# A two-block model on one core: six of nine norms scale the products instead of the operand, and the down projection lags two chunks

## What is computed

```python
def rms_norm(x, g):
    y = xf * lax.rsqrt(jnp.mean(xf * xf, axis=-1, keepdims=True) + EPS)
    return (y * g).astype(x.dtype)

def conv_ffn(h, w_up, conv_w, conv_b, w_down):   # block 1, twice (FFN 0 and 1)
    u = h @ w_up                                 # 256 x 5632
    u = conv(u, conv_w, 3 taps along tokens) + conv_b
    a, b = u[..., :D_FF], u[..., D_FF:]
    return (jax.nn.silu(a) * b) @ w_down         # D_FF = 2816

def _swiglu(x, w_in, w_out):                     # block 2, twice (FFN 2 and 3)
    gate, up = jnp.split(x @ w_in, 2, axis=-1)
    return (jax.nn.silu(gate) * up) @ w_out
```

## Time and profile before

| what | value |
|---|---|
| time, median of 3 runs | 1320.73 us (1319.76 to 1320.78) |
| span of the profiled execution, first to last instruction | 1316.1 us |
| what lies around the span (median less span) | 4.6 us |
| PE busy | 1248.9 us, 95% of the span |
| DVE busy | 844.6 us, 64% |
| ACT busy | 662.6 us, 50% |
| mean granted TensorE clock | 0.978 of full speed |

### The profile page before, as it was taken

The page is one execution under the profiler, slowest core; times in us unless marked ns, Lnnn a source line. Parts: engine busy times, 40 slices in busy tenths (PEclk is TensorE's granted clock), DMA queues, the critical chain, the costliest instruction groups (busy, mean ns, idle before and its releaser), DMA issues.

```text
span 1316.1 us, 21598 instructions
## 1 busy us (share of the span) xinstructions
PE 1248.9 (95%) x8351; PEld 1140.8 (87%) x8360; DVE 844.6 (64%) x1556; ACT 662.6 (50%) x1156; POOL 3.5 (0%) x9
## 2 busy tenths in 40 slices
PE   6999789999999889999999999999999899999996
PEld 6999768999998667899999799999899679999984
DVE  7877947666667845666766655554778855555563
ACT  6745435555546643555555534443667134344452
POOL 0000000000000000000000000000000000000000
PEclk9999979999999979999999999999999999999998
DMA  8534403554455212255455454455543134444540
GB/s 346 199 134 145 147 30 144 191 191 182 175 188 207 111 49 96 101 201 184 186 191 192 147 207 179 185 191 191 189 148 144 49 120 183 176 178 183 189 144 32
DMA packets 20433, 211.40 MB, mean 161 GB/s; under 512 B 2400, under 2 KB 2400, under 8 KB 3360
## 3 DMA queue, kind: packets, MB, share of 16 engines
q1 hardware_dynamic: 20016, 208.90, 42.9%
q0 software_dynamic: 368, 1.84, 0.4%
HBM read 209.68 MB, written 1.05 MB: 160 GB/s over the span
## 4 chain that ended last, share of the span: by engine, by line
PE 86%; DVE 8%; ACT 4%; issue 1%; DMA 1%; SPq 0%; ACTq 0%; DVEq 0%
PE ps L305 25%; PE ps L306 25%; PE ps L307 25%; PE ps L310 10%; DVE w_lo L1233 2%; ACT w_hi L812 1%; ACT arena L812 1%; DMA raw<-in_stream 1%; ACT arena L847 1%; DVE x L1299 1%; DVE arena L1729 0%; PE ps L633 0%; PE ps L468 0%; DVE arena L1323 0%; DVE arena L1547 0%
## 5 line engine op out<-in xcount | busy, mean ns | idle before, releaser
L1233 DVE TENSOR_TENSOR w_lo<-raw,w_hi 128x1024 fp32r<-128x1024 f32 (+1 forms) x390 | 444.7, 1167 | 41.3 <-ACT w_hi L812 40.6
L305 PE MATMUL ps<-h_hi,w_hi 128*128 128x256 f32 x1608 | 456.0, 284 | 0.2 <-DVE h_lo L1286 0.2
L307 PE MATMUL ps<-h_hi,w_lo 128*128 128x256 f32 x1608 | 455.0, 283 | 0.0
L306 PE MATMUL ps<-h_lo,w_hi 128*128 128x256 f32 x1608 | 455.0, 283 | 0.0
L812 ACT ACTIVATE w_hi<-raw 128x1024 fp32r<-128x1024 f32 (+1 forms) x390 | 379.1, 1007 | 6.0 <-PE ps L307 4.6
L305 PEld LDWEIGHTS ps<-h_hi,w_hi 128*128 128x128 f32 x1608 | 308.3, 192 | 3.5 <-issue 0.3
L306 PEld LDWEIGHTS ps<-h_lo,w_hi 128*128 128x128 f32 x1608 | 308.3, 192 | 3.2
L307 PEld LDWEIGHTS ps<-h_hi,w_lo 128*128 128x128 f32 x1608 | 308.3, 192 | 0.0
L305 PE MATMUL ps<-w_hi,y_hi 128*128 128x512 f32 (+2 forms) x550 | 212.1, 386 | 12.3 <-DVE y_lo L1342 5.0
L306 PE MATMUL ps<-w_lo,y_hi 128*128 128x512 f32 (+2 forms) x550 | 210.4, 382 | 0.0
L307 PE MATMUL ps<-w_hi,y_lo 128*128 128x512 f32 (+2 forms) x550 | 209.3, 381 | 0.0
(11 more groups left out here) (275 smaller groups left out, 1037.9 us busy)
## 6 DMA issues: line engine op xcount, KB each, us to landing
raw<-in_stream SPq DMA_DIRECT2D x130, 1536.0 KB, 6.3
x<-in_x SPq DMA_DIRECT2D x1, 1024.0 KB, 4.9
arena<-in_mem SPq DMA_DIRECT2D x1, 1024.0 KB, 11.9
x<-in_x POOLq DMA_DIRECT2D x1, 1024.0 KB, 5.7
out<-arena SPq DMA_DIRECT2D x4, 256.0 KB, 2.5
vec<-in_vectors SPq DMA_DIRECT2D x1, 893.0 KB, 6.6
arena<-in_final POOLq DMA_DIRECT2D x1, 512.0 KB, 5.6
arena<-in_masks SPq DMA_DIRECT2D x1, 352.0 KB, 12.0
```

Source lines behind the costliest of these rows:

```text
L305: pe.matmul(o, lh, rh, start=start, stop=False, skip_group_check=True)
L306: pe.matmul(o, lh, rl, start=False, stop=False, skip_group_check=True)
L307: return pe.matmul(o, ll, rh, start=False, stop=stop, skip_group_check=True)
L1233: dve.tensor_tensor(w_lo[:, s, a], raw[:, s, a], w_hi[:, s, a], ALU.subtract).then_inc(s_lo, 1)
```

## The change

For norms 1, 2, 3, 4, 6 and 7 (`LATE`) PE transposes `x` as it is (`turn`), in four groups, each as soon as DVE has added its part; ACT and DVE split `x * gain`; the factor is computed behind that. In an FFN the factor is spread over the partitions by two small products (`spread`, copied by ACT to `rb`), and DVE multiplies each `up` product by it (`tu`, two instructions of 128 x 256 for a chunk); convolution, silu and gate then read `tu` in SBUF instead of PSUM. After norm 2 and in the last stage the factor is the `scale` of ACT's copies and sigmoids, which were there before. `warm` and the zero products that cleared the four banks go with these six norms. Norms 0, 5 and 8 stay. In the FFNs `down` comes one chunk later (up(3), down(1), up(4), down(2), ...; after the last `up`, three downs stand instead of two). The four sums end in the order of `LAST`; in an output projection's last group the fourth sum stands behind the first `turn`. Piece 0 of a unit's weights is split one chunk earlier than before, piece 2 waits for `unit_used` by itself.

```diff
+        LATE, EARLY = (1, 2, 3, 4, 6, 7), (0, 5, 8)
+        LAST = ((0, 0), (1, 0), (0, 1), (1, 1))
+        XT_BANK = (7, 5, 6, 0)
...
 def norm(i):                                   # PE; now for 0 and 5 only
                 if i:
                     warm(WARM)
-                if i in FFN_NORM:
-                    pe.wait_ge(sem("x_done"), 4 * i)
-                    for b in range(4):
-                        full(ps[:, b, :], zero[:, :], zero[:, 0:1].to_broadcast([P, 512]))
...
 def kt_major(u, ah, al, ready, banks=(0, 1, 2, 3), norm=None):
+                        if k == KT - 1:
+                            m.then_inc(s_used if n == 3 else sem("sum_ready"), 1)
+                            if norm is not None and n == 2:
+                                turn(norm, 0)
...
+            def turn(i, n):
+                t, half = LAST[n]
+                pe.wait_ge(sem("x_done"), 4 * (i - 1) + n + 1)
+                if i == 7 and n == 0:
+                    pe.wait_ge(sem("pleT_done"), 1)
+                for k in range(4 * half, 4 * half + 4):
+                    m = pe.transpose(ps[:, XT_BANK[k // 2], ...], x[:, t, k * P:(k + 1) * P], ident)
+                    if t and k % 2:
+                        m.then_inc(sem("xT_ready"), 1)
+
+            def spread(i):
+                pe.wait_ge(sem("late_factors"), LATE.index(i) + 1)
+                for t in range(T):
+                    m = full(ps[:, 7, t * P:(t + 1) * P], NORM[:, t:t + 1].to_broadcast([P, P]), ident)
+                m.then_inc(sem("rb_ready"), 1)
...
 def ffn(i):                                    # PE
-                up(None, 0, FFN_NORM[i])
+                first_up()                     # both halves on each pair of h
+                spread(FFN_NORM[i])
+                up(None, 1)
+                up(None, 2)
+                down(None, 0)
-                with pe.Fori(0, (CH - 1) // 3) as r:
-                    for j in range(1, 4):
+                with pe.Fori(0, (CH - 4) // 3) as r:
+                    for j in range(3, 6):
                         up(r, j)
-                        down(r, j)
+                        down(r, j - 2)
+                up(None, CH - 1)
...
-                down(None, CH)
+                down(None, CH - 3)
+                down(None, CH - 2)
+                down(None, CH - 1)             # turn(0) stands before its fourth sum
+                if FFN_NORM[i] + 1 in LATE:
+                    for n in range(1, 4):
+                        turn(FFN_NORM[i] + 1, n)
...
 def late_norm(i, gain):                        # ACT
+                for n in range(3):
+                    square(n)
+                for k in range(4):
+                    high(k)
+                square(3)
+                for k in range(4, KT):
+                    high(k)
...
 def body(r, j):                                # DVE, one chunk
+                    for z in range(2):
+                        dve.tensor_tensor(tu[:, g, z * S:(z + 1) * S], ps[:, b, z * S:(z + 1) * S], rb,
+                                          ALU.mult).then_inc(sem("tu_done"), 1)
-                                m = dve.scalar_tensor_tensor(c, ps[:, b, z * S:(z + 1) * S - d], w, c,
+                                m = dve.scalar_tensor_tensor(c, tu[:, g, z * S:(z + 1) * S - d], w, c,
+                        lo(r, U0 + j + 2, 1)
                     dve.wait_ge(sem("silu_done"), at(r, n0 + j + 1))
                     dve.tensor_tensor(gg[:, g, :], sa[:, g, :], other, ALU.mult)
+                    lo(r, U0 + j + 2, 2)
                     dve.wait_ge(sem("g_hi_done"), at(r, n0 + j + 1))
                     dve.tensor_tensor(y_lo[:, g, :], gg[:, g, :], y_hi[:, g, :], ALU.subtract)
+                    lo(r, U0 + j + 3, 0)
...
 # last stage, PE
-            pe.wait_ge(sem("x_done"), 4 * 7)
...            # the small projection, now between the turns and the gate
-            norm(7)
-            pe.wait_ge(s_evac, EV[U_PROJ])
-            kt_major(U_GATE, h_hi, h_lo, lambda k: pe.wait_ge(sem("hT_ready"), 4 * 7 + k // 2 + 1))
+            pe.wait_ge(sem("hT_ready"), 4 * 7 + 4)
+            kt_major(U_GATE, h_hi, h_lo, lambda k: None, GATE_BANKS)
```

More of the change, by code:

```diff
@@ L378, in lo_at, with up_part, up @@
                     return 3 * (U0 + j) + p + 1 if r is None else r * 9 + (3 * (U0 + j) + p + 1)
-                def up(r, j, norm=None):
-                    s = (U0 + j) % SLOTS
+                def up_part(j, z, k):
+                    s, a = (U0 + j) % SLOTS, slice(z * PIECE + k * P, z * PIECE + k * P + P)
+                    return three(ps[:, 4 + j % 3, z * S:(z + 1) * S], w_hi[:, s, a], w_lo[:, s, a],
+                                 h_hi[:, k, :], h_lo[:, k, :], k == 0, k == KT - 1)
+                def up(r, j):
                     for z in range(2):
@@ L384, in up, with first_up @@
                         for k in range(KT):
+                            m = up_part(j, z, k)
+                    m.then_inc(sem("up_ready"), 1)
+                def first_up():
+                    pe.wait_ge(s_lo, lo_at(None, 0, 1))
+                    s = U0 % SLOTS
+                    for k in range(KT):
+                        if k % 2 == 0:
+                            pe.wait_ge(sem("hT_ready"), 4 * FFN_NORM[i] + k // 2 + 1)
+                        for z in range(2):
                             a = slice(z * PIECE + k * P, z * PIECE + k * P + P)
-                            if norm is not None and z == 0 and k % 2 == 0:
-                                pe.wait_ge(sem("hT_ready"), 4 * norm + k // 2 + 1)
@@ L395, in down @@
-                    pe.wait_ge(s_lo, lo_at(r, j, 2))
-                    pe.wait_ge(sem("g_lo_done"), n0 + j if r is None else r * 3 + (n0 + j))
-                    for t in range(T):
+                    s, g = (U0 + j + 1) % SLOTS, j % 3
+                    pe.wait_ge(s_lo, lo_at(r, j + 1, 2))
+                    pe.wait_ge(sem("g_lo_done"), n0 + j + 1 if r is None else r * 3 + (n0 + j + 1))
+                    for n, (t, half) in enumerate(LAST):
                         tt = slice(t * P, (t + 1) * P)
[L400 to L405, removed]
@@ L406, in down @@
-                    m.then_inc(s_used, 1)
-                up(None, 0, FFN_NORM[i])
-                pe.wait_ge(s_lo, lo_at(None, 0, 2))
-                full(ps[:, 7, 0:1], zero[:, :], zero[:, 0:1]).then_inc(s_used, 1)
-                with pe.Fori(0, (CH - 1) // 3) as r:
-                    for j in range(1, 4):
+                        a = slice(2 * PIECE + half * 512, 2 * PIECE + half * 512 + 512)
+                        m = three(ps[:, 2 * t + half, :], y_hi[:, g, tt], y_lo[:, g, tt],
+                                  w_hi[:, s, a], w_lo[:, s, a], j == 0 and r is None, True)
@@ L595, in _ @@
                     m.then_inc(sem("yT_ready"), 1)
-            kt_major(U_OUT0, y_hi, y_lo, beside_memory(0))
-            norm(1)
+            kt_major(U_OUT0, y_hi, y_lo, beside_memory(0), norm=1)
             ffn(0)
[L601 to L604, removed]
+            rows(U_MLA, 0, 384, (1, 2), h_hi, h_lo, norm=2).then_inc(s_used, 1)
+            rows(U_MLA + 1, 0, 320, (3, 4), h_hi, h_lo).then_inc(s_used, 1)
+            rows(U_MLA + 2, 0, MEM_W, (5, 0), h_hi, h_lo).then_inc(s_used, 1)
             pe.wait_ge(sem("c_done"), 1)
@@ L679, in _ @@
                     head_O(i - 3)
-            kt_major(U_OUT1, y_hi, y_lo, beside_memory(1))
-            norm(3)
+            kt_major(U_OUT1, y_hi, y_lo, beside_memory(1), norm=3)
             ffn(1)
-            norm(4)
             ffn(2)
@@ L783, in gla_y @@
                 pe.wait_ge(sem("y_ready"), KT * 2 + k + 1)
-            kt_major(U_OUT2, y_hi, y_lo, gla_y)
-            norm(6)
+            kt_major(U_OUT2, y_hi, y_lo, gla_y, norm=6)
             ffn(3)
-            pe.wait_ge(sem("pleT_done"), 1)
-            pe.wait_ge(sem("x_done"), 4 * 7)
             s = U_PROJ % SLOTS
@@ L896, in ffn @@
                     body(None, j)
-                for p in range(2):
-                    hi(None, U0 + CH + 1, p)
             def mem_kT(l):
@@ L1237, in split, with rsqrt @@
                     lo(None, u, p)
-            def rsqrt(out_, mean, n, t1, t2, scale=1.0):
+            def rsqrt(out_, mean, n, t1, t2, scale=1.0, done=None):
                 if mean is not None:
```

286 lines of the change are left out of this document (166 added, 120 removed).

## The result

The kernel after takes **1285.01 us** (median of 4, 1281.11 to 1286.43) against 1320.76 of the kernel before in the same session: a ratio of 0.9726, 95% interval 0.9713 to 0.9739, so 2.7% faster. The forecast was 1289.5, with 1278 to 1303 as its range.

The account below looks back on a forecast made before the run. PE was taken to bound the kernel inside an FFN. 13.9 + 14.7 + 6.4 - 0.4 - 3.4 = 31.2 off the span of 1316.1 gives 1284.9; plus 4.6 around it, 1289.5 us, range 1278 to 1303.

Parts of the forecast that it names:

- What bounds the kernel; the steady part: Inside an FFN PE is the bound; DVE's longer body takes 7.3 of a chunk's 8.5 us, so 0 change.
- Norms 1, 3 and 6: Behind an output projection: `up(1)` starts 4.3 us earlier at each; with 0.5 for two first downs, 13.9 gained.
- Norms 2 and 4: Behind FFN 0 and 1: the next stage starts 6.9 and 7.8 us earlier, together 14.7 gained.
- Norm 7: Before the gate: the small projection hides all of the norm's splitting, so the gate starts 6.4 us earlier.
- Norm 5: Keeps its form, but PE may now wait for the last `y_lo` before it: 0.4 us lost.
- Rival 2: At the seams, ACT's and DVE's queues hold the pairs up; gains a third shorter, 1300 us; chance 0.12.
- Rival 3: In FFN 0 and 1 DVE, not PE, sets the pace; at 9.5 us a chunk 1333; chance 0.05.
- Rival 4: At the next stage's start `w_lo` sets the pace, so lag and factor do nothing; about no change; chance 0.01.
- The clock: At the six late norms the clock falls two times of six, 1.7 us each: 3.4 us lost.
- Rival 1: The clock falls at all six norms: 1306.5 us if low through the first chunk, mild form 1296.3; chance 0.10.
- What follows it is as before: Behind the start of the gate after norm 7, the rest of the kernel was to stay unchanged.
- The base of the sum: The profiled span of 1316.1 us, with 4.6 us around it by which the median exceeds it.

Follow-up runs that it names:

- the two additions: Kernel after with two more unused 128x1024 additions on DVE in each chunk of FFN 0 and 1: 1336.79 us, ratio 1.0118.
- base: The kernel after itself, against which the experiments are compared: 1285.01 us.
- one addition: Kernel after with one more unused 128x1024 addition on DVE in each chunk of FFN 0 and 1: 1286.95 us, ratio 0.9746.
- the two of the better order: Kernel after with table early, turns behind the fourth sum, ACT alternating two squares, four high halves; the second also moves a `w_lo` piece: 1279.28 and 1278.85 us.

## Why the prediction was right, and where its numbers were off

**What bounds the kernel; the steady part.** Right. A chunk still takes 8.5 us, so the longer body costs nothing; where DVE catches up in FFN 1 it takes 7.15 us from one chunk to the next, forecast 7.3; and the two additions show how near the other side was.

```profile
559.73 0.75 DVE L1396 TENSOR_TENSOR arena<-ps,arena 128x256 f32<-128x256 f32 x2
...
566.88 0.75 DVE L1396 TENSOR_TENSOR arena<-ps,arena 128x256 f32<-128x256 f32 x2
```

**Norms 1, 3 and 6.** 4.38, 4.35 and 4.37 against 4.3. The order of events was right: PE waits 0.59 at `turn(0)`, the factor (211.16) ends before `up(0)` does. That the sums' ending part by part brings nothing here was also right, as far as the first turn goes. The 0.5 each for the first down is within the 3.48 of FFN 0 and 1. The experiment in which the first `up` waits for the factor shows the mechanism itself.

**Norms 2 and 4.** 3.48 + 4.14 = 7.62, and 3.48 + 5.67 - 0.43 = 8.72, 16.3 together; the forecast had 14.7 here and 1.0 for the first downs above, 15.7. The wait of 0.52 was forecast as 0.6, and the seams themselves, from the end of the last `up` to the next stage, took 11.75 and 11.56 where I had 11.65. Nearly all of the excess is in the 3.48 of each feed-forward, for which I had 2.73 for the down that moves and 0.5 for the first down's wait: from start to start that first down cost 0.7 more than one without a wait (`up(1)` at 216.92, the down at 223.38, against 5.75 us for the next `up`), where the row's idle time is 0.47.

**Norm 7** gained 6.54 against 6.4, with the projection hiding all of it (PE is busy for 12.00 of 12 us there). **Norm 5** cost 0.12 against 0.4.

**The rivals.** Rival 2, queues that hold the pairs up, asked for more than 12.1 us from the end of the last `up` to the next stage; it was 11.75 and 11.56. Rival 3 is what two additions a chunk make of the kernel, and it is not the kernel after. Rival 4 asked for waits for weights at the first products; the profile puts their 0.7 to 0.9 us down to `h_lo`. In "How the numbers follow", four falls and six seams each 1.3 us short make a gain of 34.6 - 6.8 - 7.8 = 20.0, where I wrote 24; neither the forecast nor the range rests on it.

**The clock** was the wrong step: I took two falls of six, 3.4 us, and none came. At norm 1 PE has 0.6 us of waiting and 0.4 of transposes ahead of the fourth sum, 1.6 of transposes and 0.9 of waiting behind it. Rival 1 did not come true in any form. With a wait of 5.56 us behind the same sixteen transposes the clock fell four times of four, and each fall cost 1.4 to 2.1 us, near the 1.7 that I had worked out. By the Trainium skill's rule that transposes do not count as busy for the clock gate ("TensorE: Matmul & The Clock Gate", Part 4) I had all six falling; the seams of this case do not bear out that use of it, and do not refute the rule either. In MLA of the kernel after, the clock fell in a stretch of the kind that I had cited against it:

```profile
416.00:420.40 4.40, 4.34 (x36) 3.99 (x35) 2.77 (x14) 1.25 (x4) 0.00 (x0) 1.00 0.49 193
420.40:424.00 3.60, 1.23 (x5) 1.14 (x5) 3.25 (x7) 3.60 (x7) 0.00 (x0) 0.80 0.00 0
424.00:428.00 4.00, 4.00 (x19) 4.00 (x18) 3.90 (x12) 0.94 (x2) 0.00 (x0) 0.75 0.63 212
```

It is the stretch from 430.50 of the earlier trace rows, with the same wait of 2.37 us for `y_lo`, where the old trace showed no fall. Over the twelve traces of this study (before, after and ten experiments) the clock fell in or behind that wait in seven. So one row without a fall was weak evidence. At the seams there was no fall at any of 42: the six of base and of each of six experiments (turns behind the fourth sum, one addition, table early, norm 5 without `warm`, the two of the better order), with waits of up to 1.66 us.

**"What follows it is as before"** was wrong by 1.4 us: the sigmoid now has a wait for the factor ahead of it, and its table load went behind the sum. I had counted the scale on the sigmoid and not the load. Why the load stands where it does was not tried further; that a sigmoid ahead of the wait takes it off the path is shown.

**The base of the sum.** I added 4.6 us around the span. In every later execution the time exceeds the span by 1.7 to 1.9. Executions of the kernel before had spans of 1315.5 to 1321.1, and the profiled one, 1316.1, was among the shortest, so the median stood 2.8 above it for that reason. The two traces differ by 33.0 us, the medians by 35.75.

Together: 1.3 better at the seams, 3.4 for falls that did not come, 2.7 for the base, less 1.4 for the tail, 1.15 for the clock elsewhere and 0.4 at the start, are the 4.5 us between 1289.5 and 1285.0. The three that made the kernel faster than forecast come to 7.4, the others to 2.95: in part they offset each other, so it is luck that the sum is off by no more than 4.5. What the model of the seams has to its credit is 34.6 against 35.9.

## What to carry to other kernels

Where a norm stands between two projections, ask which product needs the factor: a token's factor can wait for the products, and what that saves is the time between the operand and the factor, here 4.4 us at each norm behind an output projection; a wait left there can also cost clock, as the one of 5.56 us did. Such an edit moves work on to the engine that reads the sums out of PSUM, so see that its body fits in a chunk (7.2 of 8.5 here) and give it a second chunk of lag: each of the two was worth less without the other (20.2 and 7.7, together 35.8). Then look at each engine's queue at the seam, not only at the path through it: a new order of squares and high halves on ACT, one `w_lo` piece on DVE moved at three norms, and one table load brought another 0.5%.

## What the runs showed of the hardware that was not expected

- What the granted clock does at one place differs between traces that are alike there. At MLA's wait of 2.37 us it fell in seven of twelve, and at the mixer's wait of 3.00 us before its memory attention in eight of twelve. It fell at all four waits of 5.56 us, at all four of 4.03 to 4.59 (two additions a chunk) and at the one of 3.84. With one chunk of lag it did not fall at a wait of 3.24, and did at one of 2.68. It fell at none of base's six seams, where PE waits 0.92 us at most at a time.
- The mean clock varies between executions of one kernel: 0.976 to 0.981 for the kernel after, with spans of 1284.6 to 1279.3. A gain of 1 us shows in the distances of a trace, not in medians of five.
- DVE at 93% of a stretch slowed PE by nothing: 140.00 us busy of 140.
- A tap from SBUF took DVE 484 ns (255 columns) and 477 (254) against 478 and 472 from PSUM; ACT's scale and bias took 594 ns from SBUF where it had taken 561 from PSUM.
